# Four feed-forward stages of one Trainium2 kernel: the row of norm roots comes through DRAM in place of a product on TensorE

## The chip, the cores and the metric

The kernel runs on one core of one Trainium2 chip. The metric is the device time of one execution in microseconds (us). One core has five engines that run their own instruction streams and wait for one another by semaphores: TensorE (PE in the profile; PEld is its weight load), VectorE (DVE), ScalarE (ACT), GpSimd (POOL) and SyncE (SP), which here only issues transfers.

## The reference

A stack of residual blocks runs over 256 tokens of 1024 features, in float32. Between the mixers (state space with gated linear attention, latent attention, retention with pooling, and a convolution block) stand four feed-forward stages, and these are what the change touches:

```
def rms_norm(x, w):
    y = xf * lax.rsqrt(jnp.mean(xf * xf, axis=-1, keepdims=True) + NORM_EPS)
    return (y * w.astype(jnp.float32)).astype(x.dtype)
def swiglu(h, w_gate, w_up, w_down):
    return (jax.nn.silu(h @ w_gate) * (h @ w_up)) @ w_down
    ...
        x = x + swiglu(rms_norm(x, ffn_norm[i]), w_gate[i], w_up[i], w_down[i])
```

The factor `rsqrt(...)` is one number for each token, called the root below. It commutes with the products, so the kernel multiplies it onto `h @ w_gate` and `h @ w_up` after the product.

## The kernel before

All work is written out by hand as five programs, one for each engine, and their order is fixed. Every weight chunk (128 partitions x 2048 numbers, 1024 KB) is loaded by SP into one of three raw slots, split by ACT into a rounded high part (`hi`, L1165) and by DVE into the remainder (`lo`, L1681), and multiplied in three products that together have float32 accuracy. SP loads the next chunk when the `lo` of the chunk three places earlier is done.

A feed-forward stage f has 11 column blocks j of 256 hidden units. PE's order is gate 0, up 0, gate 1, up 1, down 0, gate 2, up 2, down 1 and so on. A gate or up block is `paired` (L496, then L501): its two halves take PSUM banks 0 and 1 (gate) or 2 and 3 (up). Before it writes a bank, `claim` waits until the tenant before it is `gone`. So up 1 cannot start before DVE has read the first half of up 0 out of bank 2 (the mark `f0.u0.0.gone`).

Activations stand transposed here: a hidden unit is a partition and a token is a column. The root of a token, which POOL computes as a column (`r1` by `rstd_both`: partition p holds tokens p and 128+p), is therefore needed as a row that every partition holds, `ffn.rb`. Before, DVE makes two diagonal matrices `ffn.dg` from the identity and the roots (L1689), PE multiplies a matrix of ones with them (`rstd_rows`, L797) between the two halves of up 0, and ACT copies the result from bank 4 to `ffn.rb` (L1168, with the mark `f0.rb.gone`).

For a block j, ACT copies half of the PSUM result to SBUF (`corrections`), DVE adds the other half (`add_halves`), DVE multiplies by the row (`ffn.rb2`, L1685), ACT takes the silu, DVE multiplies gate with up, ACT rounds that to `hhi` and DVE makes its remainder `hlo`, which down j needs (L467 to L469). Those products by the row are 2 for each of 11 blocks in 4 stages, 88 in all.

Of the kernel before, what the change touches and what calls it, by code (L numbers as in the profile page):

```python
# [6 lines left out]
F32 = mybir.dt.float32  # L7
# [3 lines left out]
ALU = mybir.AluOpType  # L11
# [3 lines left out]
P = 128  # L15
# [92 lines left out]
class Tally:  # L108
# [22 lines left out]
    def at(self, name):  # L131
        return self.value.get(name, (None, 0))
# [55 lines left out]
    return ap.rearrange("p (a b c) -> p a b c", a=a, b=b)  # L188


def bc(ap, shape, axis):
    return ap.unsqueeze(axis).to_broadcast(shape)

# [30 lines left out]
class FfnTiles:  # L224
    def __init__(self, arena):
        self.gr, self.ur = arena[:, 0:512], arena[:, 512:1024]
        self.sg = cut(arena[:, 1024:2048], 2)
        self.hh = cut(arena[:, 2048:3072], 2)
        self.dg, self.rb = arena[:, 3072:3328], arena[:, 3328:3584]
        self.rb2 = bc(self.rb, [P, 2, 256], 1)  # L230


class MlaTiles:
# [79 lines left out]
OUT_SLOTS = ((1, 2), (3, 4), (8, 9), (10, 11))  # L313


def build(nc, d_x, d_ws, d_cols, d_c0, d_c1, d_c2, d_gkw2, d_poolw, d_rows, d_pos, d_diag, d_out):
    ctx = ExitStack()
    with ctx:
        def sb(name, shape, dt=F32):
# [20 lines left out]
        banks = [ctx.enter_context(nc.psum_tensor(f"pb{i}", [P, 512], F32)) for i in range(8)]  # L340

        keys = [f"{e}.{s}" for e in ("pe", "act", "dve", "pool") for s in STAGES]
        keys += ["act.hi", "dve.lo"] + [f"sp.raw{i}" for i in range(NR)] + [f"sp.{n}" for n in LOADS] + ["sp.out", "act.ident"]
        tally = Tally({k: ctx.enter_context(nc.semaphore("s_" + k.replace(".", "_"))) for k in keys})
        sig, at, last = tally.sig, tally.at, tally.last
        spots = {}
# [23 lines left out]
        def bank(name):  # L370
            return banks[spots.get(name, 0)]
# [76 lines left out]
        def pe_program(e):  # L448
# [342 lines left out]
            def ffn_stage(f):  # L791
                s, key = 2 * f + 1, f"pe.ffn{f}"

                def rstd_rows():
                    b = claim(f"f{f}.rb", 4)
                    e.wait_ge(*at(f"f{f}.dg"))
                    e.matmul(b[:, 0:256], ones, ffn.dg, start=True, stop=True).then_inc(*sig(key, f"f{f}.rbm"))  # L797

                following = (lambda: turn_half(("pe.mla", "pe.ret")[f], s + 1, 0)) if f < 2 else None
                for j in range(12):  # L800
                    if j == 0:
                        opened(key, CHUNK[f"gate{f}", 0], [f"f{f}.g0.{i}" for i in range(2)], f"f{f}.gm0", s)
                    elif j < 11:
                        paired(key, CHUNK[f"gate{f}", j], [f"f{f}.g{j}.{i}" for i in range(2)], 0, f"f{f}.gm{j}")
                    if j < 11:
                        paired(key, CHUNK[f"up{f}", j], [f"f{f}.u{j}.{i}" for i in range(2)], 2, f"f{f}.um{j}",
                               rstd_rows if j == 0 else None)
                    if j == 1:
                        bs = open_out(s)
                    if j:  # L810
                        s0 = 8 + (2 * (j - 1)) % 4
                        rows_out(key, s, CHUNK[f"down{f}", j - 1], bs, (s0, s0 + 1),
                                 (f"f{f}.hlo{j - 1}.0", f"f{f}.hlo{j - 1}.1"), j == 1, j == 11,
                                 following if j == 11 else None)
# [342 lines left out]
        def act_program(e):  # L1157
# [201 lines left out]
            def ffn_stage(f):  # L1359
                s, key = 2 * f + 1, f"act.ffn{f}"  # L1360

                def corrections(name, done, out):
                    for i in range(2):
                        e.wait_ge(*at(f"{done}.{i}"))
                        run(key, f"{name}.{i}.fix", out[:, 256 * i:256 * i + 256], bank(f"{name}.{i}")[:, 256:512], ACT.Copy)

                opening(key, s, "ffn_norm" if f < 2 else "ffn_norm_g", 8 * (f % 2), CHUNK[f"up{f}", 0])
                for j in range(12):
                    if j < 11:
                        if j != 1:  # L1370
                            hi(CHUNK[f"gate{f}", j] + 2)
                        if j:
                            own()
                        corrections(f"f{f}.g{j}", f"f{f}.gm{j}", ffn.gr)
                        if j == 0:
                            e.wait_ge(*at(f"f{f}.rbm"))
                            run(key, f"f{f}.rb.gone", ffn.rb, bank(f"f{f}.rb")[:, 0:256], ACT.Copy)
                        e.wait_ge(*at(f"f{f}.g{j}"))
                        if j >= 2:
                            e.wait_ge(*at(f"f{f}.h{j - 2}"))  # L1380
                        run(key, f"f{f}.s{j}", ffn.sg[:, j % 2, :], ffn.gr, ACT.Silu)
                        hi(CHUNK[f"up{f}", j] + 2)
                        if j:
                            e.wait_ge(*at(f"f{f}.h{j - 1}"))
                        corrections(f"f{f}.u{j}", f"f{f}.um{j}", ffn.ur)
                        hi(CHUNK[f"down{f}", j - 1] + 2 if j else CHUNK[f"gate{f}", 1] + 2)
                        e.wait_ge(*at(f"f{f}.h{j}"))
                        if j >= 2:
                            e.wait_ge(*at(f"done{CHUNK[f'down{f}', j - 2]}"))
                        for i in range(2):  # L1390
                            run(key, f"f{f}.hhi{j}.{i}", ahi[:, 8 + (2 * j + i) % 4, :],
                                ffn.hh[:, j % 2, 256 * i:256 * i + 256], ACT.Copy)
                        for n in EARLY:
                            if EARLY[n] == CHUNK[f"up{f}", j] + 3:
                                hi(n)
                        for n in LOSS:
                            if LOSS[n] == CHUNK[f"up{f}", j] + 3:
                                hi(-n)
                if f > 1:
                    hi(CHUNK[f"down{f}", 10] + 2)  # L1400
                    for c in range(2):
                        squares(key, s + 1, 0, c, 4 + c)
# [267 lines left out]
        def dve_program(e):  # L1670
# [323 lines left out]
            def ffn_stage(f):  # L1994
# [10 lines left out]
                for j in range(12):  # L2005
                    if j < 11:
                        if j > 1:
                            lo(CHUNK[f"gate{f}", j] + 2)
                        add_halves(f"f{f}.g{j}", ffn.gr)
                        if j == 0:  # L2010
                            e.wait_ge(*at(f"r{s}"))
                            for t in range(2):
                                ts(key, [f"f{f}.dg"], ffn.dg[:, 128 * t:128 * t + 128], ident, st[:, 4 + t:5 + t], ALU.mult)
                            lo(CHUNK[f"gate{f}", 0] + 2)
                            e.wait_ge(*at(f"f{f}.rb.gone"))
                        own()
                        tt(key, [f"f{f}.g{j}"], cut(ffn.gr, 2), cut(ffn.gr, 2), ffn.rb2, ALU.mult)
                        lo(CHUNK[f"up{f}", j] + 2)
                        add_halves(f"f{f}.u{j}", ffn.ur)
                        own()  # L2020
                        tt(key, [], cut(ffn.ur, 2), cut(ffn.ur, 2), ffn.rb2, ALU.mult)
                        e.wait_ge(*at(f"f{f}.s{j}"))
                        if j >= 2:
                            e.wait_ge(*at(f"f{f}.hhi{j - 2}.1"))
                        own()
                        tt(key, [f"f{f}.h{j}"], ffn.hh[:, j % 2, :], ffn.sg[:, j % 2, :], ffn.ur, ALU.mult)
                        if j < 10:
                            lo(CHUNK[f"down{f}", j - 1] + 2 if j else CHUNK[f"gate{f}", 1] + 2)
                        for i in range(2):
                            slot = 8 + (2 * j + i) % 4  # L2030
                            e.wait_ge(*at(f"f{f}.hhi{j}.{i}"))
                            tt(key, [f"f{f}.hlo{j}.{i}"], alo[:, slot, :], ffn.hh[:, j % 2, 256 * i:256 * i + 256],
                               f32(ahi[:, slot, :]), ALU.subtract)
                        for n in EARLY:
                            if EARLY[n] == CHUNK[f"up{f}", j] + 3:
                                lo(n)
                        for n in LOSS:
                            if LOSS[n] == CHUNK[f"up{f}", j] + 3:
                                lo(-n)
                    if j == 10:  # L2040
                        lo(CHUNK[f"down{f}", 9] + 2)
# [400 lines left out]
        def pool_program(e):  # L2442
# [85 lines left out]
            def rstd_both(f):  # L2528
                s = 2 * f + 1
                e.wait_ge(*at(f"ss{s}.1"))  # L2530
                tt(f"pool.ffn{f}", [f"r{s}"], st[:, 4:6], st[:, 4:6], mhalf.to_broadcast([P, 2]), ALU.pow)

            ssd_stage()
            rstd_both(0)
# [183 lines left out]
```

## Time and profile before

| what | value |
|---|---|
| median of 3 runs | 1268.45 us (1268.35 to 1268.46) |
| profiled execution, its own time | 1268.46 us |
| its span in the trace | 1266.7 us |
| PE busy | 1255.7 us, 99% of the span |
| DVE, ACT, POOL busy | 72%, 57%, 8% |
| granted TensorE clock, mean | 0.999 of full speed |

The span is what the trace covers; 1.8 us of the execution's own time lie around it. The times of rows are microseconds from the start of the span. PE is the engine to read: a wait of another engine matters only where it reaches PE.

### The profile page before, as it was taken

Reading aid. Unit: us, or ns where it says so; the run is one execution under the profiler, and the core shown is the slowest. Engines: PE = TensorE matmul, PEld = TensorE weight load, DVE = VectorE, ACT = ScalarE, POOL = GpSimd, SP = SyncE. Lnnn points to the kernel's source line nnn. Section 1 sums busy time; section 2 is a strip of 40 time slices with the busy share of each in tenths; the row PEclk is TensorE's granted clock in tenths of the full one; section 3 lists DMA queues with packets and bytes.
Section 4 is the critical chain, followed back from the end, with each engine's and each line's share of the span. In section 5 each row is a group of like instructions: output and inputs, shape, how many; then the busy total and the mean of one; then the engine's idle time right before and its main releaser. Section 6 shows DMA issues by size and latency. Waiting matters only on the chain.

```text
span 1266.7 us, 17805 instructions
## 1 busy us (share of the span) xinstructions
PE 1255.7 (99%) x7056; PEld 1090.1 (86%) x7056; DVE 908.2 (72%) x1283; ACT 721.5 (57%) x1059; POOL 104.9 (8%) x137
## 2 busy tenths in 40 slices
PE   9999999999999999999999999999999999999997
PEld 8998778888888988888888888888888998888886
DVE  6967655777776685776666867877777897766665
ACT  5865454655555684754545545555555875654553
POOL 2000000000000440000000000000000781000000
PEclk9999999999999999999999999999999999999999
DMA  8443226466663313355554643686564533455551
GB/s 293 167 168 133 100 100 212 154 226 222 225 221 132 139 53 114 133 199 199 200 196 170 212 164 133 231 302 228 214 218 171 195 113 133 167 202 203 196 183 64
DMA packets 32802, 224.42 MB, mean 177 GB/s; under 512 B 3776, under 2 KB 4160, under 8 KB 7248
## 3 DMA queue, kind: packets, MB, share of 16 engines
q1 hardware_dynamic: 32576, 223.22, 50.0%
q8 instruction: 56, 0.92, 0.3%
q14 instruction: 26, 0.21, 0.1%
q10 hardware_dynamic: 144, 0.07, 0.0%
HBM read 222.23 MB, written 1.05 MB: 176 GB/s over the span
## 4 chain that ended last, share of the span: by engine, by line
PE 98%; DVE 1%; DMA 0%; ACT 0%; issue 0%; POOL 0%; ACTq 0%; SPq 0%; DVEq 0%; POOLq 0%
PE pb L496 24%; PE pb L467 16%; PE pb L468 16%; PE pb L469 16%; PE pb L501 13%; PE pb L473 3%; PE pb L1052 2%; PE pb L566 1%; PE pb L863 1%; PE pb L887 1%; PE pb L568 1%; PE pb L627 1%; PE pb L639 1%; PE pb L1111 0%; DMA xt<-d_x 0%; PE pb L694 0%
## 5 line engine op out<-in xcount | busy, mean ns | idle before, releaser
L1681 DVE TENSOR_TENSOR wlo<-raw,whi 128x2048 fp32r<-128x2048 f32 (+2 forms) x194 | 428.0, 2207 | 184.7 <-ACT whi L1165 184.3
L1165 ACT ACTIVATE whi<-raw 128x2048 fp32r<-128x2048 f32 (+1 forms) x196 | 371.9, 1899 | 63.3 <-PE pb L469 57.3
L496 PE MATMUL pb<-both,whi 128*128 128x512 f32 x1344 | 321.2, 391 | 0.0
L496 PEld LDWEIGHTS pb<-both,whi 128*128 128x128 f32 x1344 | 249.3, 188 | 49.9
L467 PE MATMUL pb<-whi,both 128*128 128x512 f32 (+2 forms) x728 | 285.6, 392 | 0.0
L468 PE MATMUL pb<-wlo,both 128*128 128x512 f32 (+2 forms) x728 | 281.6, 387 | 0.0
L469 PE MATMUL pb<-whi,both 128*128 128x512 f32 (+2 forms) x728 | 281.3, 386 | 0.0
L1168 ACT ACTIVATE arena<-pb 128x256 f32<-128x256 f32 (+1 forms) x234 | 95.7, 422 | 229.2 <-PE pb L501 149.3
L501 PEld LDWEIGHTS pb<-both,wlo 128*128 128x128 f32 x1344 | 172.3, 191 | 6.5
L501 PE MATMUL pb<-both,wlo 128*128 128x256 f32 x1344 | 174.3, 283 | 0.0
L469 PEld LDWEIGHTS pb<-whi,both 128*128 128x128 f32 x728 | 136.7, 188 | 27.9
L467 PEld LDWEIGHTS pb<-whi,both 128*128 128x128 f32 x728 | 136.9, 188 | 26.6 <-issue 1.4
L468 PEld LDWEIGHTS pb<-wlo,both 128*128 128x128 f32 x728 | 137.0, 188 | 24.2
L1685 DVE TENSOR_TENSOR arena<-arena 128x512 f32<-128x512 f32 (+3 forms) x187 | 122.2, 658 | 12.3 <-ACT arena L1168 1.3
L1685 DVE TENSOR_TENSOR arena<-arena,pb 128x256 f32<-128x256 f32 (+2 forms) x193 | 77.1, 422 | 46.1 <-ACT arena L1168 42.8
L2449 POOL TENSOR_TENSOR st<-st 128x2 f32<-128x2 f32 (+2 forms) x22 | 18.1, 824 | 883.2 <-DVE st L1694 882.5
L1168 ACT ACTIVATE arena<-arena 128x512 f32<-128x512 f32 (+6 forms) x76 | 47.4, 626 | 72.3 <-DVE arena L1685 64.8
L467 PE MATMUL pb<-both,whi 128*128 128x256 f32 (+1 forms) x280 | 80.7, 288 | 1.0 <-DVE both L1694 1.0
L468 PE MATMUL pb<-both,whi 128*128 128x256 f32 (+1 forms) x280 | 79.0, 282 | 0.0
L1168 ACT ACTIVATE both<-arena 128x256 fp32r<-128x256 f32 (+1 forms) x104 | 37.1, 396 | 51.8 <-DVE arena L1685 51.7
L1694 DVE SCALAR_TENSOR_TENSOR both<-pb,cols,both 128x256 fp32r<-128x256 f32 (+1 forms) x93 | 37.0, 455 | 31.3 <-ACT both L1168 31.3
L2449 POOL TENSOR_TENSOR arena<-arena 128x256 f32<-128x256 f32 (+3 forms) x77 | 56.7, 741 | 25.2 <-ACT arena L1168 17.0
(159 smaller groups left out, 1192.5 us busy)
## 6 DMA issues: line engine op xcount, KB each, us to landing
raw<-d_ws SPq DMA_DIRECT2D x198, 1024.0 KB, 4.9
raw<-d_ws SPq DMA_DIRECT2D x5, 768.0 KB, 4.3
arena<-d_diag SPq DMA_DIRECT2D x4, 960.0 KB, 7.6
raw<-d_ws SPq DMA_DIRECT2D x2, 576.0 KB, 3.7
arena<-d_c SPq DMA_DIRECT2D x1, 1060.0 KB, 5.0
xt<-d_x SPq DMA_DIRECT2D x2, 512.0 KB, 4.5
raw<-d_ws SPq DMA_DIRECT2D x2, 512.0 KB, 7.6
arena<-d_rows SPq DMA_DIRECT2D x2, 512.0 KB, 6.1
```

Of the source, the lines that this page charges most:

```text
L467: e.matmul(out, lh, rh, start=start, stop=False)
L468: e.matmul(out, lh, rl, start=False, stop=False)
L469: return e.matmul(out, ll, rh, start=False, stop=stop)
L473: return e.transpose(out, a, ident[0:k, 0:k])
L496: e.matmul(bs[i][:, :], wh[:, k, 128 * i:128 * i + 128], both[:, k, :], start=k == 0, stop=k == 7, skip_group_check=True)
L501: m = e.matmul(bs[i][:, 256:512], wl[:, k, 128 * i:128 * i + 128], ahi[:, k, :], start=False, stop=k == 7, skip_group_check=True)
L1165: e.activation(split_parts(n)[0], raw_part(n), ACT.Copy).then_inc(*sig("act.hi", f"hi{n}"))
L1168: e.activation(out, a, func, **kw).then_inc(*sig(key, *([name] if name else [])))
L1681: e.tensor_tensor(l[:, a:b], raw_part(n)[:, a:b], f32(h[:, a:b]), ALU.subtract).then_inc(*sig("dve.lo", f"lo{n}"))
L1685: e.tensor_tensor(out, a, b, op).then_inc(*sig(key, *names))
L1694: e.scalar_tensor_tensor(out=out, in0=a, scalar=s, in1=b, op0=op0, op1=op1).then_inc(*sig(key, *names))
L2449: e.tensor_tensor(out, a, b, op).then_inc(*sig(key, *names))
```

## The change

The diagonal matrices, the product on PE and the copy on ACT go. POOL, as soon as it has the two columns of roots, stores them to a scratch tensor `roots` in DRAM (128 rows of two numbers), waits for that transfer's semaphore, and loads the 256 numbers back to all 128 partitions in a second transfer, whose semaphore DVE waits for before the first product by the row. Both transfers are issued from POOL's own queue. The numbers come back in the order p, t in place of t, p, so `ffn.rb2` reads them with a step of two numbers and its access pattern has one dimension more.

```diff
-        self.rb2 = bc(self.rb, [P, 2, 256], 1)
+        self.rb2 = bc(self.rb.rearrange("p (a t) -> p t a", t=2), [P, 2, 2, 128], 1)
...
-                def rstd_rows():
-                    b = claim(f"f{f}.rb", 4)
-                    e.wait_ge(*at(f"f{f}.dg"))
-                    e.matmul(b[:, 0:256], ones, ffn.dg, start=True, stop=True).then_inc(*sig(key, f"f{f}.rbm"))
...
-                        if j == 0:
-                            e.wait_ge(*at(f"f{f}.rbm"))
-                            run(key, f"f{f}.rb.gone", ffn.rb, bank(f"f{f}.rb")[:, 0:256], ACT.Copy)
...
                         if j == 0:
-                            e.wait_ge(*at(f"r{s}"))
-                            for t in range(2):
-                                ts(key, [f"f{f}.dg"], ffn.dg[:, 128 * t:128 * t + 128], ident, st[:, 4 + t:5 + t], ALU.mult)
                             lo(CHUNK[f"gate{f}", 0] + 2)
-                            e.wait_ge(*at(f"f{f}.rb.gone"))
+                            e.wait_ge(*at(f"f{f}.rb"))
                         own()
-                        tt(key, [f"f{f}.g{j}"], cut(ffn.gr, 2), cut(ffn.gr, 2), ffn.rb2, ALU.mult)
+                        tt(key, [f"f{f}.g{j}"], tiles4(ffn.gr), tiles4(ffn.gr), ffn.rb2, ALU.mult)
...
                 tt(f"pool.ffn{f}", [f"r{s}"], st[:, 4:6], st[:, 4:6], mhalf.to_broadcast([P, 2]), ALU.pow)
+                e.wait_ge(*at(f"r{s}"))
+                e.dma_start(d_roots[f], st[:, 4:6]).then_inc(*sig("pool.roots", f"f{f}.roots", by=16))
+                e.wait_ge(*at(f"f{f}.roots"))
+                e.dma_start(ffn.rb, d_roots[f].rearrange("(o p) t -> o (p t)", o=1).to_broadcast([P, 256])).then_inc(
+                    *sig("pool.rows", f"f{f}.rb", by=16))
...
+    roots = nc.dram_tensor("roots", (4, P, 2), F32, kind="Internal").ap()
```

On PE, at the start of stage 0, the rows before are these: up 0 in banks 2 and 3 with the product of ones in between, then gate 1 in banks 0 and 1.

```order
L496 MATMUL pb2<-both,whi 128x512 [waits s_dve_ffn0,s_act_hi]
L496 MATMUL pb2<-both,whi 128x512 x7
L797 MATMUL pb4<-arena,c0 128x256 [waits s_dve_ffn0,s_act_ffn0]
L496 MATMUL pb3<-both,whi 128x512 [waits s_dve_ffn0]
L496 MATMUL pb3<-both,whi 128x512 x7
L501 MATMUL pb2<-both,wlo 128x256 [waits s_dve_lo]
L501 MATMUL pb2<-both,wlo 128x256 x7
```

And these after; every line number of the changed kernel is moved by a few.

```order
L500 MATMUL pb2<-both,whi 128x512 [waits s_dve_ffn0,s_act_hi]
L500 MATMUL pb2<-both,whi 128x512 x7
L500 MATMUL pb3<-both,whi 128x512 [waits s_dve_ffn0]
L500 MATMUL pb3<-both,whi 128x512 x7
L505 MATMUL pb2<-both,wlo 128x256 [waits s_dve_lo]
L505 MATMUL pb2<-both,wlo 128x256 x7
```

One product is gone, and nothing else moved. On DVE at the same place, before: the two adds of gate 0, the two diagonals, the `lo` of gate 1, the product by the row, the `lo` of up 1, the adds of up 0.

```order
L1685 TENSOR_TENSOR arena<-arena,pb 128x256 [waits s_act_ffn0] x2
L1689 TENSOR_SCALAR arena<-c,st 128x128 [waits s_pool_ffn0]
L1689 TENSOR_SCALAR arena<-c,st 128x128
L1681 TENSOR_TENSOR wlo<-raw,whi 128x2048 [waits s_act_hi]
L1685 TENSOR_TENSOR arena<-arena 128x512 [waits s_dve_lo,s_act_ffn0]
L1681 TENSOR_TENSOR wlo<-raw,whi 128x2048 [waits s_act_hi]
L1685 TENSOR_TENSOR arena<-arena,pb 128x256 [waits s_act_ffn0] x2
```

After:

```order
L1680 TENSOR_TENSOR arena<-arena,pb 128x256 [waits s_act_ffn0] x2
L1676 TENSOR_TENSOR wlo<-raw,whi 128x2048 [waits s_act_hi]
L1680 TENSOR_TENSOR arena<-arena 128x512 [waits s_dve_lo,s_pool_rows]
L1676 TENSOR_TENSOR wlo<-raw,whi 128x2048 [waits s_act_hi]
L1680 TENSOR_TENSOR arena<-arena,pb 128x256 [waits s_act_ffn0] x2
```

The diagonals are gone, and the product by the row waits for the transfer (`s_pool_rows`) where it waited for ACT. On POOL, after the root of stage 0 (the first row), two transfers are new, and the next row is POOL's work for the mixer that follows the stage.

```order
L2441 TENSOR_TENSOR st<-st 128x2 [waits s_dve_ffn0]
L2525 DMA roots<-st 128x2 [waits s_pool_ffn0]
L2527 DMA arena<-roots 128x256 [waits s_pool_roots]
L2441 TENSOR_TENSOR st<-st 128x1 [waits s_dve_mla] x2
L2449 TENSOR_SCALAR st<-st 128x2 [waits s_act_mla]
```

Before, the first row stood there with nothing between it and the work for the mixer.

## Rows read from the trace of the kernel before

**Rows 1.** The page: the span, and the chain that ended last.

```profile
span 1266.7 us, 17805 instructions
...
PE 98%; DVE 1%; DMA 0%; ACT 0%; issue 0%; POOL 0%; ACTq 0%; SPq 0%; DVEq 0%; POOLq 0%
```

**Rows 2.** Who PE waited for; total us, times, longest us.

```profile
PE pb L591 <- DVE arena L1753: 1.2, 1, 1.2
PE pb L467 <- DVE both L1694: 1.0, 1, 1.0
```

**Rows 3.** The chain around the product; start us, us, what.

```profile
232.66 1.87 PE pb L496 x8
234.53 0.43 PE pb L797 x2
234.96 1.83 PE pb L496 x8
```

**Rows 4.** The chain, a pass of sixteen that nothing interrupts.

```profile
244.26 3.65 PE pb L496 x16
```

**Rows 5.** Timeline, POOL: first and last of the four roots, and one of the end.

```profile
230.77 1.61 POOL L2449 TENSOR_TENSOR st<-st 128x2 f32<-128x2 f32 x1 [45.30 <-DVE st L1694]
...
1080.95 1.62 POOL L2449 TENSOR_TENSOR st<-st 128x2 f32<-128x2 f32 x1 [26.83 <-DVE st L1694]
1259.13 0.55 POOL L2449 TENSOR_TENSOR st<-st 128x1 f32<-128x1 f32 x1 [176.56 <-DVE st L1694]
```

**Rows 6.** Timeline, DVE in stage 0; start, us, operation, [idle before, releaser].

```profile
233.45 0.48 DVE L1689 TENSOR_SCALAR arena<-c,st 128x128 f32<-128x128 f32 x2
233.84 2.28 DVE L1681 TENSOR_TENSOR wlo<-raw,whi 128x2048 fp32r<-128x2048 f32 x1
236.23 0.69 DVE L1685 TENSOR_TENSOR arena<-arena 128x512 f32<-128x512 f32 x1
239.42 2.29 DVE L1681 TENSOR_TENSOR wlo<-raw,whi 128x2048 fp32r<-128x2048 f32 x1 [2.50 <-ACT whi L1165]
241.63 0.41 DVE L1685 TENSOR_TENSOR arena<-arena,pb 128x256 f32<-128x256 f32 x1
...
246.02 0.75 DVE L1685 TENSOR_TENSOR both<-arena,both 128x256 fp32r<-128x256 f32 x2
```

**Rows 7.** Timeline, ACT in stage 0.

```profile
235.00 0.39 ACT L1168 ACTIVATE arena<-pb 128x256 f32<-128x256 f32 x1 [1.92 <-PE pb L797]
236.95 0.63 ACT L1168 ACTIVATE arena<-arena 128x512 f32<-128x512 f32 x1 [1.57 <-DVE arena L1685]
237.49 1.90 ACT L1165 ACTIVATE whi<-raw 128x2048 fp32r<-128x2048 f32 x1
```

**Rows 8.** Timeline, TensorE: the first weight load of up 1 and of down 0.

```profile
243.98 0.31 PEld L496 LDWEIGHTS pb<-both,whi 128*128 128x128 f32 x2
...
249.55 0.19 PEld L467 LDWEIGHTS pb<-whi,both 128*128 128x128 f32 x1
```

**Rows 9.** Timeline, DVE: the first product by the row in the last stage.

```profile
1086.39 0.69 DVE L1685 TENSOR_TENSOR arena<-arena 128x512 f32<-128x512 f32 x1
```

**Rows 10.** DMA issues; times, KB each, median us from issue to landing.

```profile
raw<-d_ws SPq DMA_DIRECT2D x198, 1024.0 KB, 4.9
...
out<-arena SPq DMA_DIRECT2D x4, 256.0 KB, 2.2
...
arena<-d_c SPq DMA_DIRECT2D x1, 160.0 KB, 2.2
...
arena<-d_pos SPq DMA_DIRECT2D x1, 1.0 KB, 5.1
```

**Rows 11.** DMA view, 231.5 to 241.5 us: busy tenths in 40 slices of 0.25 us.

```profile
DMA  0000090187999999941000930979979999320000
```

**Rows 12.** Groups by form, DVE: the group that holds the products by the row.

```profile
L1685 DVE TENSOR_TENSOR arena<-arena 128x512 f32<-128x512 f32 x149 | 102.9, 692 | 10.6 <-ACT arena L1168 1.1
```

**Rows 13.** Timeline, end of stage 0: the last `hlo`, and PE's down 10.

```profile
402.52 0.76 DVE L1685 TENSOR_TENSOR both<-arena,both 128x256 fp32r<-128x256 f32 x2 [0.48 <-ACT both L1168]
...
404.30 0.39 PE L467 MATMUL pb<-whi,both 128*128 128x512 f32 x1
```

More of the change, by code:

```diff
@@ L188, in cut, with tiles4 @@
     return ap.rearrange("p (a b c) -> p a b c", a=a, b=b)
+def tiles4(ap):
+    return ap.rearrange("p (i t a) -> p i t a", i=2, t=2)
 def bc(ap, shape, axis):
@@ L313, with build @@
 OUT_SLOTS = ((1, 2), (3, 4), (8, 9), (10, 11))
-def build(nc, d_x, d_ws, d_cols, d_c0, d_c1, d_c2, d_gkw2, d_poolw, d_rows, d_pos, d_diag, d_out):
+def build(nc, d_roots, d_x, d_ws, d_cols, d_c0, d_c1, d_c2, d_gkw2, d_poolw, d_rows, d_pos, d_diag, d_out):
     ctx = ExitStack()
@@ L342, in build @@
         keys = [f"{e}.{s}" for e in ("pe", "act", "dve", "pool") for s in STAGES]
-        keys += ["act.hi", "dve.lo"] + [f"sp.raw{i}" for i in range(NR)] + [f"sp.{n}" for n in LOADS] + ["sp.out", "act.ident"]
+        keys += ["act.hi", "dve.lo"] + [f"sp.raw{i}" for i in range(NR)] + [f"sp.{n}" for n in LOADS] + ["sp.out", "act.ident", "pool.roots", "pool.rows"]
         tally = Tally({k: ctx.enter_context(nc.semaphore("s_" + k.replace(".", "_"))) for k in keys})
@@ L805, in ffn_stage @@
                     if j < 11:
-                        paired(key, CHUNK[f"up{f}", j], [f"f{f}.u{j}.{i}" for i in range(2)], 2, f"f{f}.um{j}",
-                               rstd_rows if j == 0 else None)
+                        paired(key, CHUNK[f"up{f}", j], [f"f{f}.u{j}.{i}" for i in range(2)], 2, f"f{f}.um{j}")
                     if j == 1:
@@ L2020, in ffn_stage @@
                         own()
-                        tt(key, [], cut(ffn.ur, 2), cut(ffn.ur, 2), ffn.rb2, ALU.mult)
+                        tt(key, [], tiles4(ffn.ur), tiles4(ffn.ur), ffn.rb2, ALU.mult)
                         e.wait_ge(*at(f"f{f}.s{j}"))
@@ L2714 @@
     out = nc.dram_tensor("out", (1, 256, 1024), F32, kind="ExternalOutput").ap()
-    build(nc, *args, out)
+    roots = nc.dram_tensor("roots", (4, P, 2), F32, kind="Internal").ap()
+    build(nc, roots, *args, out)
     r = _run(nc, [arrays], core_ids=[0])
```

## The prediction

> **What bounds the kernel now.** I read the page first, for the chain that ended last: PE makes 98% of it [rows 1]. The next view is who PE waits for. Its two longest entries in 1266.7 us are 1.2 and 1.0 us, each once [rows 2], and no wait of the product of ones is among them. So PE is the bound, end to end, and two things can move the time: work taken off PE, which counts in full, and a wait that some other engine now imposes on PE. The rest of the argument is about how much room there is before such a wait, and that room is read from the start of stage 0, engine by engine.
>
> **What PE loses.** The chain shows the first pass of up 0 in three pieces, 1.87, 0.43 and 1.83 us, together 4.13 us [rows 3]. The same sixteen matmuls without the product in between take 3.65 us [rows 4]. The product is thus worth 4.13 - 3.65 = 0.48 us, a little more than its own 0.43. Four stages have one each: 4 x 0.48 = 1.92 us come off PE. That is the whole possible gain, and it is 0.15% of the time.
>
> **What DVE and ACT lose.** DVE drops two diagonals, 0.48 us merged, and ACT a copy of 0.39 us for which it waited 1.92 us [rows 6, 7]. Both engines have idle time, and what DVE gains only lets the `lo` of gate 1 start about 0.4 us sooner; the work behind that `lo` is the product by the row, which waits anyway if the row is late. I price these at nothing.
>
> **The new path.** POOL has the roots at 230.77 + 1.61 = 232.38 us [rows 5]. Before, the first product by the row starts at 236.23 [rows 6], so the roots have 3.85 us to become a row with no effect on anyone. In the last stage it is 1086.39 - 1082.57 = 3.82 us [rows 5, 9]: the stages are alike, and I take stage 0 for all four.
>
> Call X the time from the roots to the row's arrival as DVE sees it. It holds a semaphore, a store to DRAM, POOL's wait for it, and a load. If X is over 3.85, DVE stands, and all the rest of its queue stands behind the product: `lo` of up 1, the adds of up 0, the remainder `hlo`. ACT stands too: its silu waits for that product, and behind the silu stands `hi` of up 1, for which DVE then waits (2.50 us of idle before the `lo` at 239.42, put down to ACT) [rows 6, 7]. The path product, silu, `hi`, `lo`, first add of up 0 has no slack in it, so each microsecond of lateness at 236.23 is a microsecond at 241.63.
>
> That add is where it meets PE. It ends at 241.63 + 0.41 = 242.04 us and frees bank 2, and PE's up 1 loads its first weights for bank 2 at 243.98 [rows 6, 8]. The room is 1.94 us before the change. PE now comes 0.48 us sooner, so 1.46 us are left. The other meeting point, `hlo` of block 0, ends at 246.77 and PE needs it at 249.55 [rows 6, 8]: room 2.78, less the 0.48 it is 2.30, so it comes second, and once PE has waited at bank 2 it is no longer late. Hence for one stage
>
> PE's new wait = X - 3.85 - 1.46 = X - 5.31, if positive, and the net is that minus 0.48: break-even at X = 5.79, and 0.2% of slowdown (2.54 us, 0.63 a stage) at X = 6.42.
>
> Behind it DVE has its idle gaps to catch up in, and the later blocks have as much room as block 1, so I add nothing for them. POOL itself has nothing else to do: its last operation before stage 0's root was 45.30 us earlier [rows 5].
>
> **How long is X?** No row shows a transfer issued by POOL, and none shows a store of 8 bytes per partition in traffic. The bounds per transfer: below, 2.2 us from issue to landing, for 256 KB to DRAM and for 160 KB from it, both on SP's queue in quiet [rows 10]. Above, 5.1 us for 1 KB behind other loads [rows 10]. The pair takes 4.4 to 10.2 us. Low end: no wait of PE, 1268.46 - 1.92 = 1266.5 us. High end: wait 4.89, net 4.41, four times: 1286.1 us.
>
> Where between? The store is issued at about 232.4 and the weight load issued just before fills the DMA engines from about 233.5 to 235.9 [rows 11]; the next one starts at about 237. The small transfers share the engines with these but don't queue behind them all, as the 1 KB load did, so I stay nearer the low end. From 2.2 I take off some 0.5 for the larger size of those rows, leaving 1.7. I add 1.0 for POOL to write the 128 or more entries of each transfer in software, and 0.6 for the traffic. Both additions are my choice. That is 3.3 for each transfer, X = 6.6, semaphores within it. The wait is 1.29, the net 0.81 a stage, and 1268.46 + 4 x 0.81 = 1271.7 us.
>
> The profiled execution's own time, 1268.46, is within 0.01 of the median of the runs, so no correction is made between them.
>
> The Trainium skill speaks against this. Its page "DMA: Bandwidth & Descriptors", section "Anatomy of one DMA - SWDGE (gpsimd) path", gives a transfer issued from GpSimd a fixed cost of about 2.0 us plus its bytes over 436 GB/s. An estimate by it is 2.0 + 2.3 = 4.3 us for the pair, and the sum would then be 1266.5 us, the second case below. The rows of SP's queue, 2.2 us with 160 KB and more, agree with such a fixed cost for that queue; none shows it for POOL's.
>
> **The strided row.** `ffn.rb2` now reads every second number. The product's group takes 692 ns for 512 numbers a partition [rows 12]; no row has that step. Below nothing; above, twice as long, 0.69 more for each of 88 products. A stage's end is where this shows: the last `hlo` ends at 403.28 and down 10 makes its first matmul at 404.30 [rows 13]. Room is about 1.0 us, and one doubled product lies in that chain. Even the upper bound just fits, so I price it at nothing and keep a small chance for it.
>
> **The rivals.**
> 1. Forecast: the row is late and PE waits at bank 2 for more than it won, X from 6.4 to 8.2. For it: two dependent transfers, each at least 2.2, against 5.3 of room. 1271.7 us; 37%.
> 2. The other side: X under 5.31. PE never waits, and the product's 0.48 is won four times: 1266.5 us. For it: both quiet rows at 2.2. It decides at 2.65 us a transfer. Against it: the weight load in flight. 24%.
> 3. X between 5.31 and 6.42: a short wait that about cancels the gain. 1267 to 1271 us; 22%.
> 4. POOL's transfers are held up. The root itself took 1.61 us where one at the end took 0.55 [rows 5]: it began under a DVE operation. If POOL's writing of the entries is held likewise, the `lo` that runs from about 233.4 to 235.7 holds the store until its end, and X is 3.3 + 3.3 + 3.3 = 9.9: net 4.11 a stage, 1284.9 us. A first use of POOL's queue that has to fetch code would act the same, once. 12%.
> 5. Doubled products that reach PE at many places: 1275 us or more, 2%. Something faster by over 0.2%, which no row offers: 3%.
>
> The page "SBUF - State Buffer" of the Trainium skill (section "SBUF: two separate sides") says that a two-input VectorE operation excludes only GpSimd operations that read SBUF, while a two-port one stops its descriptor writing. The `lo` is of the first kind, so by that rule case 4 would not happen and the time is that of case 1 or less. The trace agrees as far as the root goes, which reads SBUF and was held.
>
> **How the numbers follow.** 0.2% is about what a measurement of this kernel can tell from no change. Slower: cases 1, 4 and the 2% of 5, 51%. Same: cases 2 and 3, 46%, since the full gain is only 0.15%. Faster: 3%. The range leaves out case 4 and the strays: from 1266.3, just under case 2, to 1278.0, which is X = 8.2. The likeliest case alone spans 1271 to 1278.
>
> **What the profile after would show.** PE: sixteen matmuls of up 0 in 3.65 us without a gap. DVE: idle before the first product by the row, released by a DMA, about 2.8 us past 236.2 less the time by which all came earlier. PE: a wait of about 1.3 us before up 1 in each stage, put down to DVE's add. POOL's queue: two issues of 3.3 us to landing. What would make this wrong: transfers of 2.5 us or less, or ones of over 4; a wait of PE elsewhere than at bank 2; products longer than 0.69 us.

## The result

The changed kernel takes 1302.36 us (median of 4 runs, 1301.70 to 1302.74) against 1268.45 us before: ratio 1.0267, 95% interval 1.0254 to 1.0280. That is 33.91 us, or 8.48 us for each of the four stages. Slower was forecast, but 1271.7 us, and the range ended at 1278.0.

The page of the changed kernel, to be read against [rows 1]: the chain has 4% of DMA and 2% each of ACT and DVE in it, where PE had 98% alone, and the clock row of the 40 slices shows four dips where it had none.

```profile
span 1299.9 us, 17781 instructions
...
PEclk9999999899999999899999999899999999899999
...
PE 90%; DMA 4%; ACT 2%; DVE 2%; issue 1%; POOL 1%; ACTq 0%; SPq 0%; DVEq 0%; POOLq 0%
```

Who waited for whom (total us, times, longest us), to be read against [rows 2], where PE's longest wait was 1.2 us:

```profile
DVE arena L1680 <- DMA arena<-roots: 35.3, 4, 8.9
...
PE pb L500 <- DVE arena L1680: 26.9, 4, 6.8
POOL arena L2527 <- DMA roots<-st: 25.2, 4, 6.6
```

The chain through stage 0 of the changed kernel, in order of time (start us, us, what). L2441 is the root, L1680 on DVE the product by the row and the adds, L500 on PE the start of up 1.

```profile
230.73 1.62 POOL st L2441
...
232.65 6.54 DMA roots<-st
239.19 0.30 issue
239.49 4.99 DMA arena<-roots
...
244.50 0.70 DVE arena L1680
...
245.76 1.90 ACT whi L1163
247.66 0.02 issue
247.68 2.29 DVE wlo L1676
249.98 0.34 DVE arena L1680
250.32 0.14 issue
250.45 1.62 PE pb L500 x3
```

This is the path of the prediction, link by link: two transfers, the product, the silu (between 245.22 and 245.76, in the part left out), `hi`, `lo`, the first add of up 0, bank 2. Only the first two links are far longer than I had them: 6.54 and 4.99 us in place of 3.3 and 3.3. PE's rows at the same place:

```profile
232.45 3.85 PE L500 MATMUL pb<-both,whi 128*128 128x512 f32 x16
...
238.06 3.82 PE L500 MATMUL pb<-both,whi 128*128 128x512 f32 x16
...
250.45 5.25 PE L500 MATMUL pb<-both,whi 128*128 128x512 f32 x16 [6.67 <-DVE arena L1680]
255.54 2.08 PE L505 MATMUL pb<-both,wlo 128*128 128x256 f32 x16
```

The reader is to see two things. The pass of up 0 is whole, with nothing between its halves. And the pass after the wait lasts 5.25 us where an equal one lasts 3.82. The view by stretches shows the clock beside it (its columns: us, busy time of PE, PEld, DVE, ACT, POOL, granted clock, DMA share, GB/s):

```profile
239.00:243.00 4.00, 4.00 (x24) 3.53 (x23) 0.00 (x0) 0.00 (x0) 0.57 (x1) 1.00 0.70 203
243.00:250.40 7.40, 0.78 (x7) 0.58 (x5) 3.41 (x4) 4.77 (x5) 0.00 (x0) 0.74 0.10 32
250.40:254.00 3.60, 3.55 (x10) 2.89 (x11) 3.46 (x4) 1.38 (x4) 0.00 (x0) 0.58 0.80 280
254.00:258.00 4.00, 4.00 (x27) 3.64 (x26) 2.39 (x6) 1.54 (x2) 0.00 (x0) 1.00 0.67 223
```

While PE waits, the granted clock leaves 1.00; in the 3.6 us after it, it is 0.58 on average, mostly the lower level of 1.2 GHz, and then full again.

### The profile page after: what moved, and what is told of

The parts are those of the page before. It is cut to its first block, busy times and chain, and to the rows that moved or that the text cites. A ratio compares the mean times of both kernels' runs of the same rounds, so it can differ in the third digit from the quotient of the medians.

```text
span 1299.9 us, 17781 instructions
## 1 busy us (share of the span) xinstructions
PE 1261.4 (97%) x7048; PEld 1093.5 (84%) x7048; DVE 906.9 (70%) x1275; ACT 720.2 (55%) x1055; POOL 110.2 (8%) x145
## 4 chain that ended last, share of the span: by engine, by line
PE 90%; DMA 4%; ACT 2%; DVE 2%; issue 1%; POOL 1%; ACTq 0%; SPq 0%; DVEq 0%; POOLq 0%
PE pb L500 22%; PE pb L471 16%; PE pb L472 15%; PE pb L473 15%; PE pb L505 11%; PE pb L477 2%; DMA roots<-st 2%; PE pb L1050 2%; DMA arena<-roots 2%; ACT whi L1163 1%; ACT both L1166 1%; PE pb L861 1%; DVE wlo L1676 1%; PE pb L885 1%; PE pb L631 1%
## 5 line engine op out<-in xcount | busy, mean ns | idle before, releaser
L500 PE MATMUL pb<-both,whi 128*128 128x512 f32 x1344 | 327.1, 396 | 26.9 <-DVE arena L1680 26.9
L500 PEld LDWEIGHTS pb<-both,whi 128*128 128x128 f32 x1344 | 254.4, 192 | 79.5 <-ACT whi L1163 27.6
L472 PEld LDWEIGHTS pb<-wlo,both 128*128 128x128 f32 x728 | 137.0, 188 | 24.2
L1680 DVE TENSOR_TENSOR arena<-arena 128x512 f32<-128x512 f32 (+3 forms) x187 | 122.1, 658 | 47.6 <-DMA arena<-roots 35.3
L1680 DVE TENSOR_TENSOR arena<-arena,pb 128x256 f32<-128x256 f32 (+2 forms) x193 | 77.1, 422 | 45.8 <-ACT arena L1166 42.4
L2441 POOL TENSOR_TENSOR st<-st 128x2 f32<-128x2 f32 (+2 forms) x22 | 18.2, 827 | 885.1 <-DVE st L1689 884.4
L2441 POOL TENSOR_TENSOR arena<-arena 128x256 f32<-128x256 f32 (+3 forms) x77 | 56.9, 744 | 25.1 <-ACT arena L1166 16.9
```

The lines of the kernel that those rows point to most:

```text
L472: e.matmul(out, lh, rl, start=False, stop=False)
L500: e.matmul(bs[i][:, :], wh[:, k, 128 * i:128 * i + 128], both[:, k, :], start=k == 0, stop=k == 7, skip_group_check=True)
L1680: e.tensor_tensor(out, a, b, op).then_inc(*sig(key, *names))
L2441: e.tensor_tensor(out, a, b, op).then_inc(*sig(key, *names))
```

## The experiments

Two questions were open: why a transfer of 1 KB takes 6.5 us, and whether the wait at bank 2 is the whole loss. Each kernel has the kernel before beside it on the same chip. The first five kernels were run once each; the last four have 10 or 11 runs each.

**Both transfers from ACT's queue.** The edit takes them out of POOL's program and puts them behind ACT's copies of gate 0:

```diff
+                        if j == 0:
+                            e.wait_ge(*at(f"r{s}"))
+                            e.dma_start(d_roots[f], st[:, 4:6]).then_inc(*sig("hw.roots", f"f{f}.roots", by=16))
+                            e.wait_ge(*at(f"f{f}.roots"))
+                            e.dma_start(ffn.rb, d_roots[f].rearrange("(o p) t -> o (p t)", o=1).to_broadcast([P, 256])).then_inc(
+                                *sig("hw.rows", f"f{f}.rb", by=16))
```

> Both transfers are issued by ACT, after its copies of gate 0, in place of POOL. Theory A, traffic and the way to DRAM make the transfers long whoever issues them: store about 6 us, load about 4.5, X about 11 (in the changed kernel 12.16), time 1296 to 1301 us. Theory B, POOL's software queue makes them long: store and load about 2.5 us each, X about 5.5, no clear wait of PE, 1266 to 1270 us.

It took 1299.10 us, before 1268.22. Its DMA issues (times, KB each, median us to landing):

```profile
arena<-roots ACTq DMA_DIRECT2D x4, 128.0 KB, 4.9
...
roots<-st ACTq DMA_DIRECT2D x4, 1.0 KB, 6.5
```

Against POOL's queue in the changed kernel:

```profile
arena<-roots POOLq DMA_DIRECT2D x4, 128.0 KB, 5.0
...
roots<-st POOLq DMA_DIRECT2D x4, 1.0 KB, 6.6
```

The same, so theory B falls: beside the weight loads, POOL's queue costs next to nothing. This doesn't say what it costs in quiet, where ACT's queue was not tried.

**The load alone.** The store and the wait for it are left out, and the row comes from a weight chunk, so its values are not the roots: `e.dma_start(ffn.rb, d_ws[5, 0:1, 0:256].to_broadcast([P, 256]))`.

> The store is left out: POOL loads a row of 256 numbers from a weight chunk as soon as it has the roots, so the output is not the reference's. X should be about 0.3 + 5.0 = 5.3 us by the landing time in the changed kernel. By the formula PE's wait = X - 5.31 there is none or under 0.3 us, and the time is 1266.5 to 1267.5 us. If the load was only slow since it came behind another weight load, it is shorter here and the time is 1266.5. If the cost lay in something else than the late row (products by the row, POOL's use of the queue), the time stays above 1270.

It took 1266.64 us against 1268.22. The row is used at 237.03 us, and DVE idles only 1.32 us for it:

```profile
237.03 0.69 DVE L1680 TENSOR_TENSOR arena<-arena 128x512 f32<-128x512 f32 x1 [1.32 <-DMA arena<-d_ws]
```

So one transfer fits into the room, two don't, and 1.58 of the 1.92 us of PE's product come through. The products with the step of two numbers cost nothing extra: in the changed kernel their group still takes 692 ns, as in [rows 12].

```profile
L1680 DVE TENSOR_TENSOR arena<-arena 128x512 f32<-128x512 f32 x149 | 102.8, 692 | 45.9 <-DMA arena<-roots 35.3 <-ACT arena L1166 1.1 <-DVE arena L1680 0.5
```

**Wider pieces.** The store writes 512 bytes from each partition: `e.dma_start(d_wide[f], cols[:, 0:128])`, and the row comes from a weight chunk, so the values are not the roots.

> The store writes 512 bytes of each partition (gains and other constants) in place of 8, and the row is loaded from a weight chunk after it, so the output is not the reference's. If 8-byte pieces make the store slow, it takes 4 us or less and the time falls to about 1290 us. If they don't, it stays at 6.0 to 6.8 us and the time at 1300 to 1304 us.

1284.72 us against 1268.22. The store of 64 KB is shorter than that of 1 KB:

```profile
arena<-d_ws POOLq DMA_DIRECT2D x4, 128.0 KB, 3.6
roots<-cols POOLq DMA_DIRECT2D x4, 64.0 KB, 4.5
```

4.5 us is between the two expectations (4 or less, or over 6.0): the 8-byte pieces are worth 2.1 us in this traffic, but they are not all of it. The load fell too, from 5.0 to 3.6. It starts 2 us sooner, beside a weight load that is further on (see the next run), and it reads another place in DRAM, so its share is not cleanly told. That is also why the time fell below the 1290 us expected.

**In quiet.** SP holds the two weight loads that ran beside the transfers until the row has landed; POOL's part is unchanged.

```diff
+                for f in range(4):
+                    if old in (CHUNK[f"up{f}", 0], CHUNK[f"gate{f}", 1]):
+                        e.wait_ge(*at(f"f{f}.rb"))
```

> The two weight loads that run beside the transfers (of down 0 and gate 2) wait until the row has landed. Theory A, traffic: the store takes 3.5 us or less from issue to landing, the load too. Otherwise they keep 6.6 and 5.0. The time itself mixes this with late weights and decides nothing; with X of 7.5 and no late weights it would be 1277 us.

1279.39 us against 1268.22. The transfers:

```profile
arena<-roots POOLq DMA_DIRECT2D x4, 128.0 KB, 3.5
...
roots<-st POOLq DMA_DIRECT2D x4, 1.0 KB, 3.3
```

That is theory A: with the same bytes, pieces and queue, the store goes from 6.6 to 3.3 us once no weight load runs beside it, and the load from 5.0 to 3.5. It also tells that in full quiet the pair takes 6.8 us, above my 6.6 for a pair in traffic.

The traces also show how the traffic acts. The DMA view of the changed kernel counts packets by queue (packets, MB, share of 16 engines; q1 carries SP's weight loads, q0 POOL's transfers). The store is issued at 232.65. From 232.6 to 235.7 only q1 moves; the store's packets move from 235.7 to 236.4, together with the last ones of down 0's load:

```profile
q1 hardware_dynamic: 121, 0.99, 93.5%
...
q1 hardware_dynamic: 23, 0.06, 20.6%
q0 software_dynamic: 32, 0.00, 3.1%
```

In quiet the same 32 packets move from 233.7 to 234.0, 1.3 us after the issue at 232.44. So the small store did come behind the weight load, by 1.8 us. Most of the rest lies between its packets and its landing: 2.9 us (236.3 to 239.2) in place of 1.9 in quiet (234.0 to 235.9). The wider store's packets move at the same place, 235.7 to 236.7, and it lands at 237.05, 0.4 us after them: what the short pieces cost is this last part.

The store in turn holds the weight load behind it. From 237.5 to 239.2 nothing moves at all in the changed kernel, where the kernel before moves 313 GB/s, and gate 2's load, issued near 235.7, takes 8.4 us to landing in place of 4.8:

```profile
raw<-d_ws SPq DMA_DIRECT2D x1, 1024.0 KB, 8.4
```

It takes 8.0 us behind the store from ACT's queue too, but 4.9 beside the wider store and 5.0 without a store. POOL's load of the row, issued at 239.49, then moves its packets from 242.8 to 244.1, again around the end of that weight load (243.8). How the DMA engines come to this order is not shown.

**Keeping PE busy while it waits.** Fifteen products of constants go into free bank 4 ahead of up 1:

```diff
+                    if j == 1:
+                        b = claim(f"f{f}.warm", 4)
+                        for i in range(15):
+                            m = e.matmul(b[:, 0:256], ones, c0[:, 128:384], start=True, stop=True)
+                        m.then_inc(*sig(key, f"f{f}.warm.gone"))
```

> The changed kernel, with 15 products of constants into free bank 4 before up 1 of each stage (about 15 x 0.43 = 6.5 us of PE, inside its wait of 6.7). Theory A: of the 8.5 us that a stage lost, 6.7 are the wait, and some 2 are matmuls at the lower clock after it. Then the clock stays at its high level, the time falls by 4 x 1.5 to 2.3 us, to 1293 to 1297 us, though PE does more work. Theory B, those 2 us are something else (late weights behind the wait): the time stays at 1302 or rises.

1292.52 us against 1268.34, so 9.8 us less than the changed kernel, with more work on PE (60 matmuls more). Its chain:

```profile
243.65 6.47 PE pb L807 x30
250.13 3.65 PE pb L500 x16
```

The pass behind the filler takes 3.65 us, as in [rows 4], and the mean clock is 0.999. The arithmetic closes: 4 x (6.47 - 0.48) = 24.0 us, and 24.2 were lost. The wait that the filler stands for was 6.73 us a stage in the changed kernel, so 4 x (6.73 - 6.47) = 1.0 of the 9.8 us is a shorter wait, and 8.8 us, 2.2 a stage, are the clock. The expected time was 1293 to 1297. The clock's 2.2 is within the 1.5 to 2.3 that I gave it; the shorter wait puts the time just below.

**The transfers with nobody waiting.** The kernel before keeps its product, and POOL's two transfers are added into a spare place (`arena[:, 3584:3840]`); DVE waits for them at block 3.

> The kernel before with PE's product kept, and POOL's two transfers added into a spare place; DVE waits for them only at block 3, long after they landed. Theory A, only the wait for the row costs: 1268.2 to 1268.8 us, no change. Theory B, the transfers hold up the weight loads, and part of the loss is late weights: 1270 us or more.

1268.61 us (10 runs) against 1268.34, ratio 1.0002, interval 0.9993 to 1.0011. The transfers take 6.6 and 5.3 us here too, gate 2's weight load takes 7.4 us to landing beside them, and all this costs nothing that can be measured: the weights have the room. What costs is the wait, with the clock behind it.

**Another order around the wait.** In block 0, DVE does the `lo` of up 1, the adds of up 0 and the `lo` of down 0 before it waits for the row, and ACT its parts of them before the silu:

```diff
                             lo(CHUNK[f"gate{f}", 0] + 2)
+                            lo(CHUNK[f"up{f}", 0] + 2)
+                            add_halves(f"f{f}.u0", ffn.ur)
+                            lo(CHUNK[f"gate{f}", 1] + 2)
                             e.wait_ge(*at(f"f{f}.rb"))
...
                         corrections(f"f{f}.g{j}", f"f{f}.gm{j}", ffn.gr)
+                        if j == 0:
+                            hi(CHUNK[f"up{f}", 0] + 2)
+                            corrections(f"f{f}.u0", f"f{f}.um0", ffn.ur)
+                            hi(CHUNK[f"gate{f}", 1] + 2)
```

> The changed kernel with another order on DVE and ACT in block 0: the lo of up 1, the adds of up 0 and the lo of down 0 (and ACT's parts of them) come before the first wait for the row. Bank 2 is then free without the row. What is left behind the row is product, silu, product, hhi, hlo, about 3.5 us, and PE needs hlo at 249.1 less nothing; the row came at 244.5, so 248.0. Theory A: no wait of PE, all of the 1.9 us comes through, 1266.3 to 1267.0 us. If the earlier weight loads collide more with POOL's transfers, the row is later than 245.5 and PE waits a little at down 0: 1267 to 1272 us. Theory B, something besides bank 2 held PE: over 1275 us.

1269.23 us (11 runs, 1268.61 to 1271.42) against 1268.34: ratio 1.0010, interval 1.0001 to 1.0018. 33 of the 34 us are back, but the 1.9 are not won. The second expectation names a reason: the `lo`s that now come sooner start weight loads sooner, beside the row's load. That load went up to 7.0 us.

```profile
arena<-roots POOLq DMA_DIRECT2D x4, 128.0 KB, 7.0
roots<-st POOLq DMA_DIRECT2D x4, 1.0 KB, 6.4
```

In stage 0 the row is then used at 246.2, and in stages 1 and 3 PE waits for `hlo` at down 0, the second meeting point of the prediction. The longer of the two waits:

```profile
535.52 0.47 PE L471 MATMUL pb<-whi,both 128*128 128x512 f32 x1 [0.79 <-DVE both L1684]
```

The two waits are 1.0 us together, about half of what is missing in this run (1268.66 us, among the fastest of the eleven); the other half was not traced.

**The same order, and gate 2's weights held.** SP waits for the row before it loads gate 2, which has time.

```diff
+                for f in range(4):
+                    if old == CHUNK[f"gate{f}", 1]:
+                        e.wait_ge(*at(f"f{f}.rb"))
```

> The order of e7_reorder, and SP holds the weight load of gate 2 (and with it the ones behind it) until the row has landed, so that POOL's load of the row has the DMA engines to itself; the store still stands beside the load of down 0. Theory A: store 6.5, load 3.5 us, the row lands at about 243, and nothing waits; the 1.9 us of PE's product come through: 1266.3 to 1266.9 us, below the kernel before. If the held weights are late for ACT at gate 2 or up 2: 1267 to 1270 us. Theory B, something else costs in e7_reorder: no change against its 1269.2.

1266.71 us (11 runs, 1266.50 to 1266.93) against 1268.27: ratio 0.9987, interval 0.9978 to 0.9996. The load of the row takes 4.1 us and the store 5.6, DVE waits for the row only once, for 0.2 us, and 1.56 us of the possible 1.92 are won. In stage 0 DVE has no wait before the product by the row, the second line:

```profile
240.46 2.29 DVE L1683 TENSOR_TENSOR wlo<-raw,whi 128x2048 fp32r<-128x2048 f32 x1 [1.39 <-ACT whi L1166]
242.90 2.21 DVE L1687 TENSOR_TENSOR arena<-arena 128x512 f32<-128x512 f32 x3
```

**The order alone.** The kernel before, with PE's product, in the order of the last two.

> The kernel before, with PE's product, in the order of e7_reorder. It tells what the order alone does: 1268.2 to 1268.6 us, no change, if PE waits for nothing there now. If it falls to 1267 or less, the gain of e8_hold would be the order's and not the removed product's.

1268.21 us (11 runs) against 1268.27, ratio 1.0000, interval 0.9991 to 1.0009. The order by itself gives nothing, so the gain of the kernel above is the removed product. The held weight load was not tried by itself on the kernel before; that it adds nothing of its own is the likely reading and not shown.

## Why the prediction was wrong

**The direction: right, and by the path forecast; the size was off tenfold**, 33.9 us in place of 3.3. The prediction had named transfers of over 4 us as a sign that it would be wrong.

**What PE bounds, and what its product is worth: right.** I had 0.48 us a stage. Without a wait, 1.58 and 1.56 us came through of 1.92, 0.4 a stage.

**The meeting point and its formula: right.** I had the wait of PE as X - 5.31, with X from the roots to the first product by the row. In stage 0 of each kernel, and PE's mean wait of the four stages:

| kernel | X, us | X - 5.31 | PE's mean wait, us | lost a stage, us |
|---|---|---|---|---|
| changed | 12.16 | 6.85 | 6.73 | 8.48 |
| ACT's queue | 11.73 | 6.42 | 6.35 | 7.72 |
| wider store | 8.56 | 3.25 | 3.15 | 4.13 |
| quiet | 7.48 | 2.17 | 2.23 | 2.79 |
| load alone | 4.67 | none | 0 | -0.40 |

**The length of the transfers: wrong, and this is the step that failed.** I had 3.3 us for each transfer, made up of 1.7 in quiet, "1.0 for POOL to write the 128 or more entries of each transfer in software, and 0.6 for the traffic." In quiet they take 3.3 and 3.5, so the first two terms, 2.7 together, were 0.6 and 0.8 short. The trace doesn't support a whole 1.0 for the software: in quiet the first packets of POOL's transfers move 1.3 us after the issue, those of SP's weight load in the changed kernel 1.0 us after its own (231.82 to 232.8). The traffic term is where it broke: it is worth 3.3 us on the store (6.6 against 3.3) and 1.5 on the load (5.0 against 3.5). I had argued that a small transfer shares the engines with the weight load and doesn't queue behind it; the store's packets moved only as the weight load ended. The 5.1 us of the 1 KB load in [rows 10] was the nearer row, and even it was exceeded by the store, which I had bounded above by it. The high end of 10.2 us for the pair was thus not an upper bound: the pair took 11.5, and X, with 0.6 between the links, 12.16. With PE's measured wait of 6.73 us, the sum gives 1268.46 + 4 x (6.73 - 0.48) = 1293.5 us.

**A term that was missing: the clock.** The remaining 1302.4 - 1293.5 = 8.9 us are in the main matmuls at the lower clock behind each wait; the filler kernel shows 8.8 of it. The sum had PE start at full clock again, without saying so. What is lost beyond wait less 0.48 is 2.2, 1.9, 1.5 and 1.0 us a stage in the first four rows of the table. It shrinks because fewer of the four waits have a slow pass behind them: four, four, three (5.26 to 5.47 us) and two (5.50 us); the other passes take 3.87 to 3.91. The length of the wait alone doesn't decide it. Two stages of the quiet kernel:

```profile
812.29 5.50 PE L503 MATMUL pb<-both,whi 128*128 128x512 f32 x16 [1.97 <-DVE arena L1683]
...
1105.09 3.91 PE L503 MATMUL pb<-both,whi 128*128 128x512 f32 x16 [2.02 <-DVE arena L1683]
```

In the 3.7 us after these waits the granted clock was 0.70 and 1.00. What sets the two apart was not tried.

**The rivals.** Case 4 (the store held by DVE's `lo`) gave 9.9 for X, nearer the truth than my own, but by a mechanism that isn't seen: in the quiet kernel the store's packets move at 233.7 to 234.0, in the midst of that `lo` (233.17 to 235.45), and the same length from ACT's queue leaves no part for it. By the Trainium skill's "DMA: Bandwidth & Descriptors" (section "Anatomy of one DMA - SWDGE (gpsimd) path") a transfer issued from GpSimd has a fixed cost of about 2.0 us; even in quiet these rows show 3.3 and 3.5, so the measurement decides against using it for the sum. The Trainium skill's "SBUF - State Buffer" (section "SBUF: two separate sides") says that a two-input operation of DVE excludes a GpSimd operation that reads SBUF, and the root agrees: it takes 1.61 us, having begun under DVE's `lo`, and the same operation of the same size takes 0.69 to 0.71 us elsewhere in the trace of the kernel before. The strided row was right at nothing.

## What to carry to other kernels

Where one engine is busy for 99% of the time, a saving on it counts nearly in full (1.6 of 1.9 us here), and a new wait costs its length and, where the clock falls, the slower matmuls after it. A round trip through DRAM must be laid out against the first thing that the waiting engine's queue holds back, and not against the consumer alone. Before a small transfer is priced, look at what runs beside it: the store's latency here doubled beside 1 MB loads. When the work queued behind the wait is moved ahead of it, look also at which transfers that starts sooner.

## What was not expected of the hardware

- A store of 128 pieces of 8 bytes took 6.6 us from issue to landing beside 1024 KB loads, 3.3 us alone; one of 128 pieces of 512 bytes took 4.5 us beside the loads. The packets of both moved as the weight load in flight ended, at 235.7; the landing came 2.9 us after the last packet for the short pieces and 0.4 us after it for the wide ones.
- The store of 1 KB made the 1024 KB load issued behind it take 8.4 us in place of 4.8, from either queue; the wider store did not (4.9). Why was not tried.
- Beside the weight loads the issuing queue made no difference: 6.5 and 4.9 us from ACT's against 6.6 and 5.0 from POOL's.
- After a wait of 6.7 us of PE, the granted clock was 0.58 for the next 3.6 us, and the pass of sixteen matmuls took 5.25 to 6.75 us in place of 3.82. After two waits of 2.0 us in one kernel it took 5.50 and 3.91.
